# A hybrid two-layer block on one core: TensorE opens the scan without the band attention's store, fillers move, and two product blocks are held for the first merge

## The reference, cut to what matters

```python
def hybrid_layer(x, ...):                      # first layer
    proj = einsum('bld,dn->bln', rmsnorm(x), w_in)
    y_a = s5_mixer(u_s5, ...)
    y_b = short_conv_mixer(x_conv, b_conv, c_conv, conv_w)
    y_c = forgetting_attention(q, k, v, f_logit, b_f)
    merged = g0 * (y_a @ wa) + g1 * (y_b @ wb) + g2 * (y_c @ wc)   # g = sigmoid(gate_logits + b_gate)
    x = x + rmsnorm(merged @ w_out)
    return x + rmsnorm(relu(rmsnorm(x) @ w_ff1) ** 2 @ w_ff2)

def hybrid_mixer(h, ...):                      # second layer
    aq, ak, av, bq, bf, bi, bg, cu, cv, dx, dg, gates = split_in(h @ w_in)
    o_a = chunk_band_attention(aq, ak, av, rel_bias)
    o_b = hgrn2(bq, bf, bi, bg, lb, norm_g)    # a gated linear recurrence ("the scan")
    o_c = spatial_gating(gelu(cu), gelu(cv), norm_g, ws, bs)
    o_d = rg_lru_branch(dx, dg, ...)
    return sum(sigmoid(gates) * (stack(o_a, o_b, o_c, o_d) @ w_branch)) @ w_out

def hgrn2(q, fz, i, g, lb, norm_g):
    f = lb + (1 - lb) * sigmoid(fz); b = cumsum(log f) in blocks; kf = (1 - lb) * sigmoid(-fz)
    intra = masked scores of silu(q) * exp(b_t - b_s) * kf, times v
    inter = silu(q) * exp(b) times a state carried from block to block
    o = rmsnorm per head(intra + inter) * norm_g * silu(g)
```

## Time and profile before

| | us |
|---|---|
| median of 3 runs | 3633.23 |
| the profiled execution | 3627.11 |
| its span | 3625.6 |
| TensorE busy | 3472.5 (96%) |
| VectorE busy | 1429.7 (39%) |
| ScalarE busy | 874.9 (24%) |
| POOL busy | 905.2 (25%) |
| mean granted TensorE clock | 0.986 of 2.4 GHz |

### The profile page before, as it was taken

One profiled execution on the slowest core, in us unless ns is written; L12 is line 12 of the kernel. 1 busy time (PEld: TensorE's weight loads), 2 busy tenths in 40 slices (PEclk: granted clock), 3 DMA queues, 4 the chain that ended last, 5 costly groups with the idle time before them and its releaser, 6 DMA issues. The chain is left out here.

```text
span 3625.6 us, 40637 instructions
## 1 busy us (share of the span) xinstructions
PE 3472.5 (96%) x16148; PEld 2802.7 (77%) x16148; DVE 1429.7 (39%) x1581; ACT 874.9 (24%) x1067; POOL 905.2 (25%) x455
## 2 busy tenths in 40 slices
PE   7999999998999999999999999899999899999997
PEld 5787788887876888888867877677777688888886
DVE  7733566554324121212244436553542521121123
ACT  3222222224332111111222222212342411111112
POOL 2211111112331222222421124131254222222224
PEclk9999999999999999999999999999999999999998
DMA  3535434215412111111234222113263211111113
GB/s 120 149 95 140 142 127 136 96 70 198 162 41 76 52 46 47 46 52 46 93 111 126 86 93 93 64 64 135 93 215 127 76 46 46 46 46 52 46 46 128
DMA packets 101600, 333.40 MB, mean 92 GB/s; under 512 B 11920, under 2 KB 21520, under 8 KB 101328
## 3 DMA queue, kind: packets, MB, share of 16 engines
q1 hardware_dynamic: 100000, 326.90, 27.3%
q10 hardware_dynamic: 1472, 4.72, 0.3%
HBM read 249.06 MB, written 85.52 MB: 92 GB/s over the span
## 5 line engine op out<-in xcount | busy, mean ns | idle before, releaser
L272 POOL TENSOR_TENSOR w_lo<-w_raw,w_hi 128x1024 fp32r<-128x1024 f32 (+1 forms) x305 | 691.9, 2272 | 2547.6 <-ACT w_hi L268 2547.3
L311 PE MATMUL pair<-act_hi,w_hi 128*128 128x512 f32 x2992 | 967.4, 404 | 13.8 <-issue 7.4
L311 PE MATMUL pair<-act_lo,w_hi 128*128 128x512 f32 x2992 | 943.4, 396 | 0.0
L311 PE MATMUL pair<-act_hi,w_lo 128*128 128x512 f32 x2992 | 942.2, 396 | 0.0
L311 PEld LDWEIGHTS pair<-act_lo,w_hi 128*128 128x128 f32 x2992 | 564.6, 189 | 138.2
L311 PEld LDWEIGHTS pair<-act_hi,w_lo 128*128 128x128 f32 x2992 | 563.4, 188 | 137.7
L311 PEld LDWEIGHTS pair<-act_hi,w_hi 128*128 128x128 f32 x2992 | 545.2, 189 | 133.9 <-issue 15.9
L268 ACT CAST w_hi<-w_raw 128x1024 fp32r<-128x1024 f32 x275 | 288.4, 1049 | 970.7 <-PE pair L311 911.3
L594 DVE TENSOR_TENSOR p<-pair,rs 128x1024 f32<-128x1024 f32 x100 | 122.3, 1223 | 410.9 <-PE pair L311 398.7
L1832 DVE TENSOR_TENSOR f2v<-pair,rs 128x1024 f32<-128x1024 f32 x42 | 51.5, 1225 | 346.5 <-PE pair L311 346.5
L311 PE MATMUL pair<-f1hl,w_hi 128*128 128x512 f32 x480 | 147.8, 389 | 0.0
(11 more groups left out here) (471 smaller groups left out, 3966.9 us busy)
## 6 DMA issues: line engine op xcount, KB each, us to landing
w_raw<-in_stream SPq DMA_DIRECT2D x276, 512.0 KB, 3.6
proj<-p SPq DMA_DIRECT2D x101, 512.0 KB, 2.6
m2g<-proj SPq DMA_DIRECT2D x32, 512.0 KB, 4.6
foxx<-proj SPq DMA_DIRECT2D x32, 256.0 KB, 5.7
m1g<-proj SPq DMA_DIRECT2D x16, 512.0 KB, 3.3
x<-f1y SPq DMA_DIRECT2D x16, 512.0 KB, 2.6
act_lo<-x SPq DMA_DIRECT2D x16, 512.0 KB, 6.7
n1x<-in_x ACTq DMA_DIRECT2D x8, 512.0 KB, 9.1
```

The costliest lines, as they stand in the source:

```text
L272: last = nc.gpsimd.tensor_tensor(wlo[:, slot, at:at + n], raw[:, slot, at:at + n], whi[:, slot, at:at + n].bitcast(F32), ALU.subtract)
L311: last = nc.tensor.matmul(out_pair[:, h * HALF:(h + 1) * HALF], wt, a[:, h * HALF:(h + 1) * HALF], start=k == 0 and n_pass == 0, stop=k == ...
```

## The change

In the scan, TensorE no longer waits at the start on band_read; instead every use of its PSUM banks waits for VectorE's last instruction of the attention. The other engines no longer wait for the attention's store: only SP does, before the loads of the second half, and the buffers of the second half are laid out where the store reads from. A new argument `between` of `spread_inv_sqrt` issues points behind the reciprocal. Points are added and moved: four before the first scores of each half, five instead of three in `state`, two between the norm's halves and four instead of five behind it; in the gating branch four between and two behind instead of four behind. The numbers of expected points follow: 152 for 140 in the scan and 84 for 82 in what comes after. In the first layer, 16 tiles are kept back instead of 8; the turned splits and 8 of the held tiles are issued ahead of the merge's opening, and the splits of operands 4 to 7 ahead of the last 7 tiles.

```diff
-    def spread_inv_sqrt(rstd, scale, mark, g=1, rows=False):
+    def spread_inv_sqrt(rstd, scale, mark, g=1, rows=False, between=None):
...
         v = V.mark(V.after(a).reciprocal(t_, t_))
+        if between:
+            between()
...
-        band_read = [V.last(), A.last(), PE.last(), stores[0].last(), *(s.last() for s in bias_load)]
+        band_read, band_out = [V.last(), A.last(), PE.last(), *(s.last() for s in bias_load)], stores[0].last()
...
-            sets = [[sb(at, f"hg_{n}{i}", [P, L]) for n in ("q", "v", "g", "k", "b")] for i in range(2)]
+            sets = [[sb(at, f"hg_{n}0", [P, L]) for n in ("q", "v", "g", "k", "b")]]
...
+            sets.append([sb(at, f"hg_{n}1", [P, L]) for n in ("q", "v", "g", "k", "b")])
...
-            for engine in (nc.vector, nc.scalar, nc.gpsimd, nc.tensor, SP):
+            for engine in (nc.vector, nc.scalar, nc.gpsimd, SP):
...
-            bank_read = [[None, None], [None, None]]
+            bank_read = [[band_read[0], band_read[0]], [band_read[0], band_read[0]]]
...
+                if i:
+                    SP.wait_ge(*band_out)
                 for buf, row in zip((f, *sets[i][0:4]), (BF, BQ, BI, BG)):
...
                 factors(0, exponents(0))
+                point(4)
...
-                point(3)
+                point(5)
                 done = transposes(kt, ...)
...
-                spread = spread_inv_sqrt(qd, 1.0 / HD, token_sums(kd, a, heads[:, 0:P:HD]), g=2)
+                spread = spread_inv_sqrt(qd, 1.0 / HD, token_sums(kd, a, heads[:, 0:P:HD]), g=2, between=lambda: point(2))
                 bank_read[0] = [spread, spread]
-                point(5)
+                point(4)
...
-        r = spread_inv_sqrt(rstd, 1.0 / 256, sums, rows=True)
-        point(4)
+        r = spread_inv_sqrt(rstd, 1.0 / 256, sums, rows=True, between=lambda: point(4))
+        point(2)
         ops.split(0, 2)
...
-            w.again(FOX_HEADS * 24 + 8, KT)
+            w.again(FOX_HEADS * 24 + 8, 2 * KT)
...
+            for r in range(4):
+                ops.split_turned(r, 8 + r)
+            A.after(ops.ready[3])
+            w.upto(w.done + KT)
             merging = merge(ops, proj1, GATE1, 3, ...)
             next(merging)
-            for r in range(4):
-                ops.split_turned(r, 8 + r)
-            A.after(ops.ready[3])
+            ops.split(4, 8)
         advance(n, n)
-        ops.split(4, 8)
         next(merging)
...
-                w.again(140, 12 * KT)
+                w.again(152, 12 * KT)
                 freed = hgrn(hgrn_const, stored)
             ops = Operands(at, 8, "m2")
-            w.again(82)
+            w.again(84)
```

## The result

The changed kernel takes 3599.49 us, the median of 4 runs (3595.73 to 3606.95); beside it the kernel before took 3633.28 us (3633.01 to 3633.37). The ratio is 0.9913, with a 95% interval of 0.9901 to 0.9925: by the medians 33.8 us faster (the interval allows 27 to 36), where 38.9 were forecast. The profiled execution took 3598.66 us, with a span of 3597.0, 28.6 less than before.

What follows compares the result with a forecast made beforehand. TensorE, busy 3472.5 of 3625.6 us, was taken as the bound, so gains are its idle or slow-clock time. Terms 7.8 + 1.0 + 7.9 + 9.9 + 6.3 + 7.5 - 1.5 = 38.9 us give 3594.3 us; range 3580 to 3618.

Steps and rivals of the forecast that it cites:

- Part 1: Scan opening: without TensorE's wait the first scores start earlier, with 23 tiles behind them for 20; gain 7.8 us (4 to 10).
- Part 2: Scan levels, both halves: fewer waits on VectorE's factor chain; first half gains 1.0 us (-3 to +3).
- between the halves: Before the second half's first scores: 8 tiles and two transposes cover VectorE's chain; gain 7.9 us (5 to 9).
- second half: Second half's levels: evictions move and ten tiles precede the first transpose, 3.1 of 13.0 us remain; gain 9.9 (5 to 11).
- Part 3: Gating branch's norm: five tiles between root and spread remove the "tok" wait and others; gain 6.3 us (5 to 7).
- Part 4: First merge: 8 more held tiles cover the wait for split operands, 4.7 us remain; gain 7.5 us (2 to 11).
- Part 5: First attention: 8 tiles fewer over 200 points, mostly covered; costs 1.5 us (bounds +1 and -8).
- Rival D: Scan opening: VectorE or POOL ends the same hole, added points only move waits; 3630 us, chance 0.04.
- The formula: Scan-level idle: 7.75 + 1.4j - 1.4m (eviction before masks), 2.6 - 1.4k (before exponents); j, k, m tiles ahead, behind, in level.
- A: Scan levels give the gain back: every level waits another 1.3 us, 16 us in all; 3610 us, chance 0.15.
- B: First merge gains nothing: gates land 5 us later and the second slow start returns; 3602 us, chance 0.12.
- C: Attention and scan bound by their own chains, so tiles taken out leave holes; slower, 3642 us, chance 0.03.

Runs made afterwards that it cites:

- experiment 10: Changed kernel with 194 instead of 200 expected points in the first attention, restoring the old pace; 3594.34 us, ratio 0.9888.
- experiment 3: Changed kernel with a base target of four tiles more; the program came out the same, instruction for instruction; 3602.57 us, ratio 0.9921.
- experiment 2: Kernel before with only the first layer's edits (16 tiles held, turned splits and held tiles ahead of the merge); 3639.89 us, ratio 1.0025.
- 12: Changed kernel with 194 expected attention points, three scan points ahead of the cumulated sums, ScalarE's merge guard behind the held tiles; 3590.34 us, ratio 0.9885.
- Experiment 4: Changed kernel with three of the eight points at the scan's opening moved between logarithms and cumulated sums; 3598.12 us, ratio 0.9911.
- 11: Changed kernel with the first layer as before and three of eight scan-opening points ahead of the cumulated sums; 3591.45 us, ratio 0.9887.
- Experiment 6: Changed kernel with TensorE again waiting at the scan's opening for the attention's last instructions and store; 3604.44 us, ratio 0.9918.
- Experiments 7: Changed kernel with the points between root and spread of the three norms put behind the spread again; 3610.43 us, ratio 0.9937.
- experiments 9: Changed kernel with the four new points before each half's first scores put behind those scores; 3614.09 us, ratio 0.9944.
- Experiment 5: Changed kernel with six more tiles run before the first attention, so evictions fall elsewhere; 3608.89 us, ratio 0.9929.

## Why the prediction was right, and where it was not

The total came within 5.2 us, and part of that is luck: the errors had both signs, and the profiles, from which the terms were read, gained only 28.6 us. Each term as the prediction put it, against the two profiled executions (start of an instruction less 1.40 us for each product tile done by then):

| | forecast | measured | from |
|---|---|---|---|
| Part 1, opening | +7.8 | +4.1 | first scores, 23 tiles for 20 |
| Part 2, first half | +1.0 | +2.3 | to L1484, 69 tiles for 68 |
| between the halves | +7.9 | +7.3 | first scores of the second half |
| second half | +9.9 | +12.5 | to the gating branch's sums |
| Part 3, gating norm | +6.3 | +8.8 | to the second merge |
| Part 4, first merge | +7.5 | +7.2 | attention's end to the next wait |
| Part 5, attention | -1.5 | -13.8 | counted as in experiment 10 |
| elsewhere | 0 | 0.0 | +1.5 ahead of the attention, -2.9 at the norms (1060 to 1140), -0.5 from there to the scan, +1.9 behind |
| sum | 38.9 | 28.4 | span: 28.6 |

The profiled execution gained 28.6 us and the medians 33.8, because the one profiled before (3627.11) lay 6.2 us below its median and the changed one (3598.66) 0.8 below its own. The changed kernel's executions lie 11 us apart; so do those of the kernel before in the experiments' batches (3626.24 to 3637.34 in the first), though beside the result they lay within 0.4. The terms are of one execution each. In experiment 3's, of the same program, Part 1 is 2.8, the first half -0.8 and the merge 7.7; between the halves, the second half and the attention come out as in the table. So the first half's +2.3 isn't established.

Of the signs that the prediction named, three for "right" held or nearly held: no wait on "tok", a clock of 0.99 in the scan's stretch, and 15.9 us idle there for 13. Two didn't: one wait at the opening is 4.76 us, and the merge waits for a weight unit and not for the ninth operand. One sign for "wrong" came, 20 us idle in the first attention: it is 21.4.

**The step that failed is Part 5's,** "most steps have cover to spare; where they have none a step loses 3 x 0.04 x 1.4 = 0.17 us. Over some nine bare steps that is 1.5 us". It measured 13.8, outside its lower bound of 8 as well. I had priced the tiles that a step loses and not the evictions that move when the rate changes, although the prediction itself says of the scan that their place matters more than the number of tiles. In the attention I never listed them. At the rate of before they fall in the steps of query blocks 1, 3, 5 and 7 (counted from 0), in nearly every head; at 1.285 a point they fall in those of 0, 2, 4 and 6 for seven heads, where the one in block 4's step stands behind the reciprocal (3.35) and the next head's split. In four of these heads the weight unit's subtraction on POOL, which moves along, also falls on L717. Experiments 2, 10 and 12 show it: 7.1 us slower with this part alone, and 9.9 of the 13.8 gone when the rate is put back. The wrong base (121 for 135) shifts all places too, but I had not used them. Most of the 9.9 is the slowed L717: 2.07 us more in each of four heads, 8.3 in all. No run moved the one without the other, as they come with the same tile, but the heads in which only the eviction is there show its share, waits of 0.8 to 0.9 us. The other 3.9 us are the eight tiles themselves, at the attention's end.

**Part 1** has the right hole and the right second cause, and missed a third. The sum of 3.7 us for waits behind the opening was 6.1 (1.34 and 4.76). My list of what is late next had the splits of units 21 and 22. It had not the eviction of the 9th tile, queued on VectorE behind a scan of 4.32 us. Experiment 4 moved it and won 3.5 us by the trace, and 11 repeated that. The loads came 2.65 us earlier where I had 2.2. Experiment 6 shows how little the removed wait is worth alone: by its waits 7.9 against 4.8 + 1.3, and by the path to L1429 1.4 us, inside the scatter. Rival D ("the waits reappear one operation on") was half true of this part.

**Parts 2 and 3** held. The formula's 3.55 us at level 2 is 3.34 in the trace, its 1.2 us with one tile behind the eviction 1.06 (at 2374.59), and the first scores of the second half wait no more. The 3.1 us left for the waits of that half are 2.5 (0.95, 0.49 and 1.06). Its clock gave more than I had: the prediction counted 3.5 us of slow clock in the levels before, but from the first scores to L1484 the granted clock rose from 0.94 to 1.00, which is worth 5.9 us of the 98.65. One wait was mis-sized: at the heads' product of the first half it is 2.49 us for 1.3. "tok" is gone, as is L1564's wait. Experiments 7 and 9 put the two groups of points back and lost 7.0 and 8 to 10 us locally. The granted clock of the scan's stretch went from 0.95 to 0.99. In the profile the busy time fell by 12.1 us with the same matmuls, out of 28.6 gained. The Trainium skill, "TensorE: Matmul & The Clock Gate", Part 1, puts the ramp's penalty under 1% of a typical span. The 12.1 us agree with that, being 0.3% of this span, and yet a sum that is to tell a gain of 1% can't leave them out.

**Part 4** has the right size, 7.2 for 7.5, by a different remainder. Of the forecast's 4.7 us only a wait of 2.85 and its slow tiles are there. The first gate opened at 855.24 against a forecast of 853.8, and the ninth operand is in time all the same in this execution. In experiment 3's it is waited for 0.88 us and in experiment 2's 2.28, so it is a matter of when the gates land. What I missed is the guard on ScalarE ahead of the weight cast.

The rivals: A (levels give it back), B (nothing at the merge) and C (slower) did not come. C's mechanism did, in one place: "a tile taken out of them leaves a hole" is the 3.9 us at the end of experiment 10's attention. A's slowed subtraction cost most in the attention, where the prediction had not looked for it.

## What to carry to other kernels

When filler work is handed out along a straight line, a change of its rate moves every side effect that hangs on a tile (here the eviction on VectorE, the cast on ScalarE, the subtraction on POOL), so list where these fall in each step before and after, for every stage whose rate changes, and look for steps in which a chain on that engine already bounds, or in which the moved work on POOL would run beside a subtraction on VectorE. If work must be held back, take it off the end and keep the rate. When a wait of the busiest engine is removed, ask of each buffer that it will reach earlier who frees it and what stands ahead of that in its queue.

## What was not expected of the hardware

- The same hole doesn't always cost the same. In the changed kernel L1429 stands behind a wait of 2.49 us and took 1.98. Experiment 3's kernel issues the same instructions, its waits in the scan are the same to 0.1 us, and there it took 3.54:
```profile
2215.35 3.54 PE L1429 MATMUL bank<-hg_o,hg_heads 128*128 128x512 f32 x4 [2.50 <-DVE hg_o L1426]
```
The granted clock from L1429 to L1484 was 1.00 in the one and 0.96 in the other, and the stretch took 79.3 and 82.5 us. At the merge a wait of 2.85 us is followed by a pair of matmuls at 1.22 us (granted clock 0.50, the 1.2 GHz level), and one of 3.04 us (experiment 10) by one at 0.73 (1.00). So the length of a hole doesn't settle by itself whether the clock falls to 1.2 GHz. These 3.2 us are a large part of the 4.4 by which the two spans differ (3597.0 and 3601.4). Whether the clock explains all of the 11 us between executions of one kernel wasn't tested.
- VectorE's subtraction L717 on 64 partitions takes 1.22 us alone and 3.29 beside POOL's 2.44 us subtraction. The Trainium skill, "SBUF — State Buffer", section "SBUF: two separate sides", says that the two share a port pair which the first holds for its whole instruction, and the 2.07 us more agree with it, as POOL had started 0.24 us earlier. Experiment 5 shows the other order: in head 0 L717 started 0.10 us ahead of POOL (358.80 and 358.90), kept its 1.22 us, and POOL's subtraction took 3.33.
- The waits of a stage repeat when its order of instructions is the same, and its time mostly does: the attention took 504.9 us in the changed kernel and in experiments 2, 3, 4 and 7, which have its rate, and 495.0 in both with the paced one. But not always: experiments 9 and 6 have the same code there and the same 17.6 us of waits on L787, and took 507.7 and 508.9 us, at a granted clock of 0.99.
